# Element scatters that signal three semaphores in turn, with a wait for the third scatter ahead

## The reference

```python
s1 = einsum('thd,hkd->thk', q1, keys_a); s2 = einsum('thd,hkd->thk', q2, keys_b)
v1, i1 = top_k(s1, 16); v2, i2 = top_k(s2, 16)
top_s, pos = top_k(v1[..., :, None] + v2[..., None, :], 16)   # 8 heads x 16 picks of 128*128 experts
gates = softmax(top_s)
act = gelu(h . expert_u[idx]);  y = sum over picks of gates * act * expert_v[idx]
```

## Time and profile before

| | |
|---|---|
| median of three runs | 1535.73 us (1531.17 to 1535.74) |
| the profiled execution | 1541.21 us |
| its span, first to last instruction | 1539.3 us |
| mean granted TensorE clock | 0.99 |
| PE busy | 1491.1 us (97% of the span) |
| DVE busy | 1225.4 us (80%) |
| ACT busy | 690.2 us (45%) |
| POOL busy | 503.9 us (33%) |
| HBM traffic over the span | 277 GB/s |

### The profile page before, as it was taken

One profiled execution on the slowest core, in us unless ns is written; L12 is line 12 of the kernel. 1 busy time (PEld: TensorE's weight loads), 2 busy tenths in 40 slices (PEclk: granted clock), 3 DMA queues, 4 the chain that ended last, 5 costly groups with the idle time before them and its releaser, 6 DMA issues.

```text
span 1539.3 us, 22283 instructions
## 1 busy us (share of the span) xinstructions
PE 1491.1 (97%) x7643; PEld 1305.1 (85%) x7643; DVE 1225.4 (80%) x2474; ACT 690.2 (45%) x1191; POOL 503.9 (33%) x439
## 2 busy tenths in 40 slices
PE   7999998999999999999989999999999999999997
PEld 4786666889989899999979999988888888888886
DVE  6775656477789798999869786678898888888886
ACT  5424756354444343434436554344444344434443
POOL 0000000001475678667667867311111111112100
PEclk8999999999999999999989999999999999999999
DMA  9693913045787576766768999999999999999992
GB/s 363 236 361 124 409 41 128 1 147 219 237 277 237 172 252 209 224 194 189 241 207 298 323 335 352 377 358 384 368 382 386 370 380 388 373 373 370 371 346 108
DMA packets 169904, 427.46 MB, mean 278 GB/s; under 512 B 21152, under 2 KB 105280, under 8 KB 149824
## 3 DMA queue, kind: packets, MB, share of 16 engines
q1 hardware_dynamic: 143168, 291.67, 54.6%
q0 software_dynamic: 26624, 134.37, 22.9%
HBM read 373.42 MB, written 52.56 MB: 277 GB/s over the span
## 4 chain that ended last, share of the span: by engine, by line
PE 74%; another core or an unknown queue 1%; DVE 1%; ACT 1%; issue 1%; DMA 1%; SPq 0%; ACTq 0%; DVEq 0%
PE ps_y L2119 11%; PE ps_y L2123 11%; PE ps_y L2121 11%; PE ps_u L1183 11%; PE ps_u L1185 11%; PE ps_u L1184 11%; PE ps_g L1816 2%; PE ps_q L1470 2%; PE ps_q L1472 2%; PE ps_q L1471 2%; DMA activations<-u_act 1%; PE ps_s L1482 1%; PE ps_u L2154 0%; ACT u_act L1193 0%
## 5 line engine op out<-in xcount | busy, mean ns | idle before, releaser
L1462 POOL DMA_INDIRECT gate_tiles<-gate_owed,gate_cell x256 | 339.2, 1325 | 133.5 <-issue 72.6
L1183 PE MATMUL ps_u<-h_hi,u_hi 128*128 128x384 f32 x1024 | 348.4, 340 | 10.5 <-ACT u_act L1193 8.1
L1185 PE MATMUL ps_u<-h_hi,u_lo 128*128 128x384 f32 x1024 | 346.1, 338 | 2.3 <-issue 2.2
L1184 PE MATMUL ps_u<-h_lo,u_hi 128*128 128x384 f32 x1024 | 345.7, 338 | 2.0 <-issue 1.8
L1243 POOL DMA_INDIRECT row<-in_uv_rows,row_index x128 | 157.4, 1229 | 525.1 <-DVE y_row L1266 445.7
L1990 ACT CAST v_hi<-v_raw 128x1024 fp32r<-128x1024 f32 x128 | 134.8, 1053 | 273.9 <-DMA v_raw<-in_v 124.8
L2119 PE MATMUL ps_y<-v_hi,w_hi 128*128 128x512 f32 x768 | 237.9, 390 | 0.3 <-DVE w_lo L2037 0.3
L2123 PE MATMUL ps_y<-v_hi,w_lo 128*128 128x512 f32 x768 | 237.1, 389 | 0.0
L2121 PE MATMUL ps_y<-v_lo,w_hi 128*128 128x512 f32 x768 | 237.0, 389 | 0.0
L1173 DVE TENSOR_TENSOR u_lo<-u_raw,u_hi 128x1024 fp32r<-128x1024 f32 x128 | 155.2, 1218 | 83.8 <-ACT u_hi L1166 65.5
L1183 PEld LDWEIGHTS ps_u<-h_hi,u_hi 128*128 128x128 f32 x1024 | 193.6, 189 | 14.3 <-issue 13.0
(11 more groups left out here) (320 smaller groups left out, 2079.6 us busy)
## 6 DMA issues: line engine op xcount, KB each, us to landing
u_raw<-in_u SPq DMA_DIRECT2D x128, 512.0 KB
v_raw<-in_v SPq DMA_DIRECT2D x128, 512.0 KB
activations<-u_act SPq DMA_DIRECT2D x128, 192.0 KB
gates<-gate_tiles SPq DMA_DIRECT2D x32, 768.0 KB, 9.9
w_ada<-in_w_ada SPq DMA_DIRECT2D x23, 1024.0 KB, 7.4
gate_tiles<-blank SPq DMA_DIRECT2D x4, 4096.0 KB, 30.2
act<-activations SPq DMA_DIRECT2D x64, 192.0 KB
u_act<-activations SPq DMA_DIRECT2D x64, 192.0 KB
```

The costliest lines, as they stand in the source:

```text
L1183: pe.matmul(out, self.hi[n][:, k], hi, start=(k == 0), stop=False)
L1184: pe.matmul(out, self.hi[n][:, k], lo, start=False, stop=False)
L1185: last = pe.matmul(out, self.lo[n][:, k], hi, start=False, stop=(k == KD - 1))
L1462: pool.indirect_dma_start(out=g_dram, out_offset=bass.IndirectOffsetOnAxis(ap=picks.cell[:, b, j:j + 1], axis=0), in_=picks.owed[:, b, j:j ...
```

## The change

There are three semaphores in place of `spread`. Scatter m, counted over all turns, adds to number m mod 3. From the fourth scatter on, each one that doesn't start a turn waits until its own semaphore shows that scatter m-3 has landed (`spread_by(m, r)` is how many of the first m scatters signal number r). The first of a turn waits, as before, for all scatters before it, now on three semaphores, and so does SyncE at block 121. Scatters, gathers, their order and their data stay.

```diff
+IN_FLIGHT = 3
+
+
+def spread_by(m, r):
+
+    return (m - r + IN_FLIGHT - 1) // IN_FLIGHT
...
         def spread_gate(pool, g, n):
 
-            b, j = n // TOPK, g * TOPK + n % TOPK
+            b, j, m = n // TOPK, g * TOPK + n % TOPK, g * SPREADS + n
             if n == 0:
                 pool.wait_ge(picks.summed, g + 1)
                 if g > 0:
-                    pool.wait_ge(spread, 16 * SPREADS * g)
+                    for r in range(IN_FLIGHT):
+                        pool.wait_ge(spread[r], 16 * spread_by(m, r))
+            elif m >= IN_FLIGHT:
+                pool.wait_ge(spread[m % IN_FLIGHT], 16 * spread_by(m, m % IN_FLIGHT))
             pool.indirect_dma_start(out=g_dram, out_offset=bass.IndirectOffsetOnAxis(ap=picks.cell[:, b, j:j + 1], axis=0),
-                                    in_=picks.owed[:, b, j:j + 1], in_offset=None).then_inc(spread, 16)
+                                    in_=picks.owed[:, b, j:j + 1], in_offset=None).then_inc(spread[m % IN_FLIGHT], 16)
...
                     if i == -OPENING:
                         for n in range(2):
                             sp.wait_ge(g_stored[n], 16 * (P // G_TOK // 2))
-                        sp.wait_ge(spread, 16 * SPREADS * PEER_HEADS)
+                        for r in range(IN_FLIGHT):
+                            sp.wait_ge(spread[r], 16 * spread_by(SPREADS * PEER_HEADS, r))
                         load_gates(0)
                         load_v(0)
...
-        spread = top.enter_context(nc.semaphore("gates_spread"))
+        spread = [top.enter_context(nc.semaphore(f"gates_spread{n}")) for n in range(IN_FLIGHT)]
```

## The result

The changed kernel takes 1598.97 us (median of four runs, 1595.11 to 1601.26) against 1534.22 us: a ratio of 1.043, with a 95% interval of 1.041 to 1.046, some 65 us. The profiled execution, with a span of 1593.1 us against 1539.3, shows 53.8 us of it; all that follows is told on these spans. The two differ because the profiled execution of the kernel before was 7.0 us slower than its median (1541.2 against 1534.2) and that of the changed kernel 3.9 us quicker than its own. Forecast were 20 us.

What follows compares the result with a forecast made beforehand. TensorE's matmuls were 74% of the chain, with Pool the late engine in turns 6 and 7. The last scatter 26 us later, less 5.7 us of early `u_lo`, gave 20 us on 1535.7: 1556 us, range 1531 to 1580 us.

Steps and rivals of the forecast that it cites:

- SyncE's wait: At block 121, for the last scatter: a 26 us delay costs 9 us this way, not added to the rows.
- The signs that I had named for the waits: Pool waits for scatters 40 to 60 times, 50 to 90 us together; VectorE waits for rows tens of us.
- Rival C: Pool's lateness adds up from turn 3 on, last row 50 us late, TensorE stalls: 1580 us and up; chance 0.10.
- the delay of the last scatter: End of Pool's scatters: last one starts 26 us later, taken from bounds of 8 to 50 us.
- The replay itself: Pool's DMA list, each scatter held until the third ahead landed: last starts 22 us later, 50 with 1.2 us lag.
- second replay: Pool's queue with packets 15% and start 20% quicker: last scatter 8 us later without lag, 16 us with.
- The step on the early turns: Turns 0 to 5: 32 us of unmet waits, absorbed by waits for row buffers in the replay.
- The 5.7 us of early `u_lo`: Before product 124: `u_lo` was 5.7 us early, so 20 of 26 us reach TensorE.
- Rival A: Pool's queue is quick enough, scatters land within 3.8 us or the slack hides the delay: 1536 us; chance 0.20.
- Rival B: TensorE's holes around 510 and 785 us come from Pool's queue; thinning it gives 12 us back: 1524 us; chance 0.10.

Runs made afterwards that it cites:

- run 1: Changed kernel with three semaphores but without the wait for the third scatter ahead: 1.000 of the kernel before.
- run 2: Changed kernel with as many waits on Pool, each for a count already met: 1.001 of the kernel before.
- run 6: Kernel before, with SyncE at block 121 also waiting until TensorE has done product 125: 1.0055 of the kernel before.
- run 9: Kernel before with no row used between blocks 24 and 122; no total time given, scatters land 3.4 us after start on average.
- run 10: Changed kernel with no row used between blocks 24 and 122; no total time given, first v product 3.9 us earlier than in the same-paced kernel before.
- run 7: Kernel before with rows used more slowly while the scatters run: 1.014 of the kernel before.
- run 12: Changed kernel with the new wait in turns 4 to 7 alone: 1.021 of the kernel before.
- run 5: Changed kernel with two scatters in flight instead of three: 1.108 of the kernel before.
- run 8: Changed kernel with rows used more slowly while the scatters run: 1.037 of the kernel before.
- run 11: Changed kernel with the new wait in turns 0 to 3 alone: 1.005 of the kernel before.

## Why the prediction was wrong

**What was right.** That the wait isn't always met; that neither the semaphores nor the wait instructions cost anything (runs 1 and 2); that rows are the way to TensorE and SyncE's wait is not (the waits in the trace, runs 6, 9 and 10); that nothing is won back in the v stage. The signs that I had named for the waits came, and stronger: 70 waits and 131 us on Pool where I had said 40 to 60 and 50 to 90, 108 us on VectorE where I had said tens. Half of the 108 us come before 925 us, the first at 761. Rival C, the lateness adds up from turn 3 on and some 50 us or more come through, is what happened.

**The term that was mis-sized** is the delay of the last scatter: 26 us, measured 55.5. The replay itself, with 1.2 us of lag and the packet times as they were, had given 50. I had pulled it down with a second replay in which packets are 15% and the start of the queue 20% quicker, because late Pool "thins the traffic". That rested on no row. Measured in the changed kernel, while the scatters run: a gather keeps the queue for 3.33 us on average instead of 3.39, a scatter 0.59 us instead of 0.64, so all of them together keep it 5% less. In turns 6 and 7 it is some 10% (3.27 us instead of 3.63 for a gather), but run 1, without the waits, has 3.36 us there. And the lag that I had from four cases, 0.9 to 1.9 us, is 1.29 us in the median of the 65 scatters that Pool held for landing, read in steps of 0.25 us (1.4 us by the packets' own ends). The bounds were 8 and 50 us; taking the middle of bounds of which one has rows behind it and the other an assumption was the mistake.

**The step on the early turns** failed too. I had let the waits for row buffers swallow what turns 0 to 5 lose, and had sized that loss at 32 us by the count without lag. With the lag of 1.2 us the same count gives some 80 us there (63 scatters of 184), as much as in turns 6 and 7. In the changed kernel turn 3 starts 16.2 us late, turn 4 19.7, turn 5 24.9, turn 6 22.3, turn 7 38.6 us late. Only between turns 5 and 6 is a little given back. The first late rows come in turn 4, at 761 us, near block 84, just where VectorE begins to use rows at more than twice the pace.

**The 5.7 us of early `u_lo`** hide nothing, though it may look so in the sum (55.5 - 53.8). Counted from block 83, where it was 8.7 us ahead, TensorE loses 53.0 + 8.7 = 61.7 us, more than the last scatter does. The slack was counted at the wrong door. TensorE waits for ACT's gelu, which stands behind the row's weight in ACT's program, with two PSUM banks between, and once for VectorE's one-hots. That it hardly ever waits for `u_lo` is shown (0.3 us). Of the 61.7 us, 49.3 are waits and 12.4 are the same matmuls at a lower granted clock; the sum of the prediction had nothing for the clock, which stood in rival C alone.

**Rival A and the Trainium skill's 2.0 us** ("DMA: Bandwidth & Descriptors", section "Anatomy of one DMA"): here the mean from start to landing is 4.2 us, and 3.4 us even without gathers in front. Only the quickest, from 1.7 us on, are within the page's figure. The page gives it as the fixed cost of one DMA; the time behind other DMAs of the queue comes on top of it here.

**Rival B**: the hole near 510 us is indeed not there in the changed kernel, and it was 8.7 us ahead at block 83. The other traces bear B out in part. `u_lo` of block 36 starts at 525.4 to 528.1 us in the kernel before and in runs 1, 2, 6, 7 and 12, where in the first turns no scatter but the first of a turn waits for a landing. It starts at 518.7 to 521.6 us in the changed kernel and in runs 5, 8 and 11, at 523.3 us with four or six in flight, and at 517.8 and 518.8 us in runs 9 and 10, without rows. So what Pool issues there has a part in the hole, and holding its scatters back or taking its gathers away gives some 4 to 9 us back. By what way isn't shown, and the later loss is several times as large.

**What stays open** besides: how much of the 55.5 us is the spread of the traces. Against runs 1 and 2 the last scatter is 38 to 46 us late; the ratio of 1.043 is of medians and doesn't hang on it.

## What to carry to other kernels

A limit on DMAs in flight is free while there is room, and steep below. Here scatters start 1.28 us apart at the quickest, and the mean from start to landing with the lag of the waiting engine is some 5.5 us (4.2 + 1.3). Six in flight span 7.7 us and cost nothing that can be measured, although the slowest landing takes 9.8 us; four span 5.1 us and cost 0.4%; three span 3.8 us and cost 4.3%; two span 2.6 us and cost 10.8%. That the limit has to span the mean landing with its lag fits these four numbers; no other kernel was tried. Count what else goes through the same queue: the large gathers among the small scatters lengthen the landing from 3.4 to 4.2 us, and what waits behind the scatter on the issuing engine sets the price. Follow the lateness through every engine that has the late item in its program, here ACT as well as VectorE, before you count slack. If you replay a queue, use the rows as they are, and don't discount them by an effect that no row shows.

## What the runs showed of the hardware that I had not expected

The issuing engine goes on about 1.3 us (median of 65) after the count of packets shows the DMA that it waits for to be through. With three in flight and 1.28 us between issues this lag alone is one whole issue. And in the v stage, where the DMA engines had a share of 0.99 already, 13 more row gathers (57 - 44 by block 128) of 1 MB weren't free: with them the stage took 27 us longer (563.3 - 536.5).
